# The end of a decoder step: the last down rows in smaller transfers, the last expert sums kept in PSUM, the output turned before it is normalised

## The reference

```python
h2 = rmsnorm(x, g_ffn) * (1 + sc2) + sh2
x = x + gt2 * moe(h2, w_router, b_router, w_gu, b_gu, w_d, b_d)   # 32 experts, 4 for each token
...
y_prompt = rmsnorm(xp, g_final)     # (1, 256, 1024)
y_sample = rmsnorm(xs, g_final)     # (8, 1, 1024)

def rmsnorm(x, g):
    y = x * lax.rsqrt(jnp.mean(x * x, axis=-1, keepdims=True) + RMS_EPS)
    return y * g
```

## Time and profile before

| | us |
|---|---|
| median of 3 runs | 1345.26 (1340.6 to 1347.05) |
| the profiled execution | 1347.29 |
| its span, first to last instruction | 1345.7 |
| PE busy | 1222.4 (91%) |
| DVE, ACT, POOL busy | 317.3, 175.4, 48.8 |
| moved by DMA | 500.51 MB, mean 372 GB/s |
| last weight transfer lands | 1304.48 |
| from there to the end of the span | 41.2 |

### The profile page before, as it was taken

The page is one execution under the profiler, slowest core; times in us unless marked ns, Lnnn a source line. Parts: engine busy times, 40 slices in busy tenths (PEclk is TensorE's granted clock), DMA queues, the critical chain, the costliest instruction groups (busy, mean ns, idle before and its releaser), DMA issues.

```text
span 1345.7 us, 15198 instructions
## 1 busy us (share of the span) xinstructions
PE 1222.4 (91%) x5950; PEld 608.0 (45%) x5950; DVE 317.3 (24%) x566; ACT 175.4 (13%) x341; POOL 48.8 (4%) x93
## 2 busy tenths in 40 slices
PE   5999998999999989899898989898998989898886
PEld 2788755688443433424242434334342424334234
DVE  2379855332112020111101110210111011102103
ACT  2132231100210100200010010001000100200002
POOL 0121231000000000000000000000000000000000
PEclk9899999999998999999999999998999999999988
DMA  9998999963699999999999999999999999999970
GB/s 353 328 349 302 376 314 364 395 261 138 250 422 414 373 417 409 418 406 420 407 413 414 419 415 418 418 415 420 380 421 415 392 415 420 417 416 419 403 296 34
DMA packets 105951, 500.51 MB, mean 372 GB/s; under 512 B 8514, under 2 KB 10672, under 8 KB 70161
## 3 DMA queue, kind: packets, MB, share of 16 engines
q1 hardware_dynamic: 99136, 478.37, 88.8%
q0 software_dynamic: 6496, 21.42, 4.6%
q10 hardware_dynamic: 272, 0.09, 0.0%
HBM read 496.48 MB, written 3.38 MB: 371 GB/s over the span
## 4 chain that ended last, share of the span: by engine, by line
PE 72%; DMA 23%; ACT 2%; DVE 1%; issue 1%; SPq 1%; DVEq 0%
PE ps L924 25%; DMA ring<-in_w_d 21%; PE ps L431 11%; PE ps L966 10%; PE ps L982 4%; PE ps L824 4%; PE ps L874 3%; PE ps L365 3%; PE ps L794 2%; PE ps L749 2%; DMA ring<-in_w_ada 2%; PE ps L396 1%; PE ps L605 1%; ACT oT L1265 1%; PE ps L890 1%
## 5 line engine op out<-in xcount | busy, mean ns | idle before, releaser
L924 PE MATMUL ps<-ring,zone 128*64 128x512 f32 x2032 | 443.0, 592 | 2.0 <-issue 2.0
L966 PE MATMUL ps<-ring,oT 128*64 128x512 f32 x1024 | 254.2, 654 | 73.5 <-DMA ring<-in_w_d 73.5
L924 PEld LDWEIGHTS ps<-ring,zone 128*64 128x64 f32 x2032 | 147.8, 137 | 289.2 <-issue 286.8
L966 PEld LDWEIGHTS ps<-ring,oT 128*64 128x64 f32 x1024 | 79.4, 150 | 247.4 <-issue 166.5
L1795 DVE TENSOR_SCALAR zone<-ps 128x1024 f32<-128x1024 f32 x16 | 19.6, 1225 | 631.3 <-PE ps L924 631.3
L431 PE MATMUL ps<-hT,ring 128*128 128x264 f32 x640 | 152.5, 397 | 2.1 <-DVE hT L1384 1.8
L431 PEld LDWEIGHTS ps<-hT,ring 128*128 128x128 f32 x640 | 123.1, 195 | 29.6 <-issue 6.6
L1260 ACT ACTIVATE attn<-zone 128x1024 f32<-128x1024 f32 x16 | 16.9, 1057 | 502.9 <-DVE zone L1795 502.8
L1812 DVE TENSOR_TENSOR zone<-zone,ps 128x264 f32<-128x264 f32 x64 | 27.5, 430 | 190.0 <-PE ps L982 190.0
L824 PE MATMUL ps<-zone,dec_scores 128*64 128x512 f32 x256 | 58.7, 599 | 0.0
L365 PE MATMUL ps<-ident,zone 128*128 128x128 f32 (+3 forms) x212 | 32.0, 277 | 15.9 <-DMA zone<-in_b_alpha 10.4
(11 more groups left out here) (340 smaller groups left out, 761.4 us busy)
## 6 DMA issues: line engine op xcount, KB each, us to landing
ring<-in_w_gu SPq DMA_DIRECT2D x127, 2048.0 KB, 17.6
ring<-in_w_d SPq DMA_DIRECT2D x64, 2048.0 KB, 15.6
ring<-in_w_ada SPq DMA_DIRECT2D x12, 2048.0 KB, 12.7
ring<-in_w_in SPq DMA_DIRECT2D x9, 2048.0 KB, 13.4
ring<-in_cache_k SPq DMA_DIRECT2D x32, 256.0 KB, 7.7
ring<-in_cache_k POOLq DMA_DIRECT2D x32, 256.0 KB, 6.7
ring<-in_cache_v SPq DMA_DIRECT2D x32, 256.0 KB, 10.5
ring<-in_cache_v POOLq DMA_DIRECT2D x32, 256.0 KB, 9.0
```

The costliest lines, as they stand in the source:

```text
L924: ins = pe.matmul(ps[64 * j:64 * j + CAP, c, :], xg[:, k, 2 * par + j, :], rows, start=False, stop=(k == KT - 1), skip_group_check=True)
L966: ins = pe.matmul(ps[64 * j:64 * j + CAP, 4 + c, :], hidT[:, k, j * CAP:(j + 1) * CAP], w[j][:, kk, c * 512:(c + 1) * 512], start=(k == 0) ...
```

## The change

The change rewrites all that follows the last quad, on four engines, in a function `finish` for each of PE, ACT and DVE, and `load_last` for SP.

- **Loads.** Of the last four `w_d` transfers, i = 0 and 1 stay. Instead of i = 2 and 3 (2 MB each), SP issues eight transfers of 512 KB, one for each of 4 row blocks and 2 experts, row block by row block, once both slots are free. PE waits for each row block alone (`late0` to `late2`, and `landed` for the last).
- **Sums in banks.** DVE adds `modT * acc` of the first seven quads to `xT` ahead of time, and clears banks 0 to 3 and 64 columns of bank 6. PE accumulates the last quad's sums in those banks: blocks m = 2b and 2b + 1 of the prompt in bank b (256 columns each), all sample columns in bank 6 (8 for each m). The products of par 0 and the samples' of par 0 come before `down(last, 1)`, those of par 1 behind it. DVE then does one operation for each m: `xT = ps * modT + xT`. `ye_tok[1]` is taken out in two halves, the first of them while PE computes the second.
- **g_final by rows.** PE spreads `g_final` over the partitions (`final_row`, two times four products of a broadcast column with the identity, bank 7), ACT copies it to `g_row`.
- **Output.** PE transposes `xT` (x2 unscaled) to token rows in banks 4, 5, 7, 0 (prompt) and 1, 2 (samples). ACT squares each bank with a sum along the row; DVE adds the two halves' sums, ACT takes the root (mean and epsilon within it), DVE the reciprocal, [128, 2] and [8, 1]. DVE then writes the output from the banks: bank times reciprocal of the token times `g_row`. SP stores in three transfers (256 tokens in two, then the samples), and the read of the number of rounds on DVE lies behind it.

The diff, without the removed lines that stand in the kernel above, and without the declarations of the new tiles (`g_row`, `squares_of`, `x2_ss`, `x2_inv`, `eps_col`, and `y_tok`, which lies over `hT`):

```diff
+        Y_BANKS = (4, 5, 7, 0, 1, 2)
...
-            def down(q, par, edge, cold):
+            def down(q, par, edge, cold, rnd=0):
 
                 n = q * 2 + par
                 if not cold:
                     pe.wait_ge(sig("ye_ready"), n)
                 for s in range(2):
                     pe.wait_ge(sig("read"), q * 10 + (5 + 2 * par + s))
-                    w = [expert_slot("dn", 2 * s + j, n, edge)[:, 0:4096].rearrange("p (k c) -> p k c", k=4)
-                         for j in range(2)]
+                    by_rows = edge and s == 1
+                    if by_rows:
+                        w = [ring[:, expert_load("dn", 2 * s + j, n, edge)[1], 0:4096]
+                             .rearrange("p (k c) -> p k c", k=4) for j in range(2)]
+                    else:
+                        w = [expert_slot("dn", 2 * s + j, n, edge)[:, 0:4096].rearrange("p (k c) -> p k c", k=4)
+                             for j in range(2)]
                     for kk in range(4):
                         k = 4 * s + kk
+                        if by_rows and kk < 3:
+                            pe.wait_ge(sig(f"late{kk}"), rnd * 32 + 32)
+                        elif by_rows:
+                            for j in range(2):
+                                expert_slot("dn", 2 * s + j, n, edge)
                         for c in range(2):
                             for j in range(2):
                                 ins = pe.matmul(ps[64 * j:64 * j + CAP, 4 + c, :], hidT[:, k, j * CAP:(j + 1) * CAP],
@@ -968,15 +980,76 @@
                                                 start=(k == 0), stop=(k == KT - 1), skip_group_check=True)
                                 if kk == 3 and c == 1:
                                     ins.then_inc(sig("slots_used"), 1)
-
-            def combine(q, last):
+                                elif by_rows and kk == 3:
+                                    ins.then_inc(sig("down_half"), 1)
+
+            def final_row(rnd, g):
+
+                if g == 1:
+                    pe.wait_ge(sig("g_taken"), rnd * 2 + 1)
+                for k in range(4):
+                    col = vecT[:, VEC_ROWS["g_final"][0] + 4 * g + k:VEC_ROWS["g_final"][0] + 4 * g + k + 1]
+                    ins = pe.matmul(ps[:, 7, k * P:(k + 1) * P], col.to_broadcast([P, P]), ident[:, :],
+                                    start=True, stop=True)
+                ins.then_inc(sig("g_filled"), 1)
+
+            def final_products(par, m):
+
+                return pe.matmul(ps[:, m // 2, (m % 2) * TP:(m % 2 + 1) * TP], ye_tok[par][:, m * P:(m + 1) * P],
+                                 putT[:, par, 0:TP], start=False, stop=(par == 1), skip_group_check=True)
+
+            def final_samples(par):
+
+                for m in range(KT):
+                    ins = pe.matmul(ps[:, 6, m * NS:(m + 1) * NS], ye_tok[par][:, m * P:(m + 1) * P],
+                                    putT[:, par, TP:T], start=False, stop=(par == 1), skip_group_check=True)
+                return ins
+
+            def final_turns(rnd, q):
+
+                for g in range(2):
+                    for t in range(2):
+                        for k in range(4):
+                            m = 4 * g + k
+                            if t == 0 and k % 2 == 0:
+                                pe.wait_ge(sig("added"), q * KT + (KT + m + 2))
+                            ins = transpose(ps[:, Y_BANKS[2 * g + t], k * P:(k + 1) * P],
+                                            xT[:, m, t * P:(t + 1) * P])
+                        ins.then_inc(sig("x2_turned"), 1)
+                pe.wait_ge(sig("x2_samples"), rnd + 1)
+                for g in range(2):
+                    for k in range(4):
+                        ins = transpose(ps[0:NS, Y_BANKS[4 + g], k * P:(k + 1) * P], xT[:, 4 * g + k, TP:T])
+                    ins.then_inc(sig("x2_turned"), 1)
+
+            def finish(rnd, q):
+
+                pe.wait_ge(sig("read"), q * 10 + 10)
+                final_row(rnd, 0)
+                pe.wait_ge(sig("sums_ready"), rnd + 1)
+                pe.wait_ge(sig("ye_ready"), q * 2 + 1)
+                for m in range(KT):
+                    final_products(0, m)
+                final_samples(0)
+                final_row(rnd, 1)
+                down(q, 1, True, False, rnd)
+                pe.wait_ge(sig("ye_half"), rnd + 1)
+                for m in range(KT):
+                    if m == 4:
+                        pe.wait_ge(sig("ye_ready"), q * 2 + 2)
+                    final_products(1, m).then_inc(sig("summed"), 1)
+                final_samples(1).then_inc(sig("samples_summed"), 1)
+                pe.wait_ge(sig("g_taken"), rnd * 2 + 2)
+                final_turns(rnd, q)
+
...
-                down(q + (QUADS - 1), 1, True, False)
-                combine(q + (QUADS - 1), True)
+                finish(rnd, q + (QUADS - 1))
...
+            def finish(rnd, q):
+
+                for g in range(2):
+                    act.wait_ge(sig("g_filled"), rnd * 2 + (g + 1))
+                    nc.scalar.activation(g_row[g], ps[:, 7, :], ACT.Copy).then_inc(sig("g_taken"), 1)
+                act.wait_ge(sig("sums_ready"), rnd + 1)
+                nc.scalar.activation(eps_root, eps_col, ACT.Sqrt)
+                act.wait_ge(sig("down_half"), rnd * 2 + 2)
+                nc.scalar.activation(ye_tok[1][:, 0:512], ps[:, 4, :], ACT.Copy).then_inc(sig("ye_half"), 1)
+                act.wait_ge(sig("slots_used"), down_done(q * 2 + 1, True))
+                nc.scalar.activation(ye_tok[1][:, 512:1024], ps[:, 5, :], ACT.Copy).then_inc(sig("ye_ready"), 1)
+                for n in range(6):
+                    rows = P if n < 4 else NS
+                    if n == 4:
+                        act.wait_ge(sig("x2_sums"), rnd * 2 + 1)
+                        nc.scalar.activation(x2_inv[:, 0:2], x2_inv[:, 0:2], ACT.Sqrt, bias=eps_col[:, 0:1],
+                                             scale=1.0 / D).then_inc(sig("x2_roots"), 1)
+                    act.wait_ge(sig("x2_turned"), rnd * 6 + (n + 1))
+                    nc.scalar.activation(squares_of[n], ps[0:rows, Y_BANKS[n], :], ACT.Square,
+                                         accum_out=x2_ss[0:rows, n:n + 1]).then_inc(sig("x2_sq"), 1)
+                act.wait_ge(sig("x2_sums"), rnd * 2 + 2)
+                nc.scalar.activation(x2_inv[0:NS, 2:3], x2_inv[0:NS, 2:3], ACT.Sqrt, bias=eps_col[0:NS, 0:1],
+                                     scale=1.0 / D).then_inc(sig("x2_roots"), 1)
+
...
-                add_quad(q + (QUADS - 1))
-                dve.wait_ge(sig("added"), q * KT + (QUADS * KT + KT))
+                finish(rnd, q + (QUADS - 1))
+
+            def finish(rnd, q):
+
+                for bank in range(4):
+                    ins = V.memset(ps[:, bank, :], 0.0)
+                V.memset(eps_col, EPS)
+                dve.wait_ge(sig("added"), q * KT + KT)
+                for m in range(KT):
+                    V.scalar_tensor_tensor(out=xT[:, m, 0:TP], in0=acc[:, m, 0:TP], scalar=modT[:, 40 + m, 0:1],
+                                           in1=xT[:, m, 0:TP], op0=ALU.mult, op1=ALU.add)
+                chain(V.tensor_tensor(acc[:, :, TP:T], acc[:, :, TP:T], modT[:, 40:40 + KT, 1:9], ALU.mult))
+                chain(V.tensor_tensor(xT[:, :, TP:T], xT[:, :, TP:T], acc[:, :, TP:T], ALU.add))
+                dve.wait_ge(sig("read"), q * 10 + 9)
+                V.memset(ps[:, 6, 0:KT * NS], 0.0).then_inc(sig("sums_ready"), 1)
+                for m in range(KT):
+                    if m % 2 == 0:
+                        dve.wait_ge(sig("summed"), q * KT + (KT + m + 2))
+                    V.scalar_tensor_tensor(out=xT[:, m, 0:TP], in0=ps[:, m // 2, (m % 2) * TP:(m % 2 + 1) * TP],
+                                           scalar=modT[:, 40 + m, 0:1], in1=xT[:, m, 0:TP], op0=ALU.mult,
+                                           op1=ALU.add).then_inc(sig("added"), 1)
+                dve.wait_ge(sig("samples_summed"), rnd + 1)
+                sums = ps[:, 6, 0:KT * NS].rearrange("p (k b) -> p k b", b=NS)
+                chain(V.tensor_tensor(qk_new, sums, modT[:, 40:40 + KT, 1:9], ALU.mult))
+                V.tensor_tensor(xT[:, :, TP:T], xT[:, :, TP:T], qk_new, ALU.add).then_inc(sig("x2_samples"), 1)
+
+                def inverse(rows, t0, n, first, number):
+                    dve.wait_ge(sig("x2_sq"), rnd * 6 + first + 2 * n)
+                    V.tensor_tensor(x2_inv[0:rows, t0:t0 + n], x2_ss[0:rows, first:first + n],
+                                    x2_ss[0:rows, first + n:first + 2 * n], ALU.add).then_inc(sig("x2_sums"), 1)
+                    dve.wait_ge(sig("x2_roots"), rnd * 2 + number)
+                    chain(V.reciprocal(x2_inv[0:rows, t0:t0 + n], x2_inv[0:rows, t0:t0 + n]))
+
+                def scaled(out, rows, t, n, g):
+                    V.scalar_tensor_tensor(out=out, in0=ps[0:rows, Y_BANKS[n], :], scalar=x2_inv[0:rows, t:t + 1],
```

(38 more changed lines are left out.)

65 lines of the change are left out of this document (21 added, 44 removed).

## The result

| | before | after |
|---|---|---|
| median (9 runs each) | 1345.4 (1340.6 to 1347.05) | **1333.38** (1331.8 to 1340.77) |
| the profiled execution, and its span | 1347.29, 1345.7 | 1335.32, 1333.7 |
| PE busy | 1222.4 | 1216.4 |

The ratio is 0.9932, 95% interval 0.9915 to 0.995: 0.7% faster. The forecast was 1333.9. The parts behind that agreement are less exact, and some of their errors cancel.

The account below looks back on a forecast made before the run. Weight stream and PE were nearly matched; the chain of waits behind the last quad decided. `down` ending at 1315.6 plus 18.65 gave 1334.3 against 1345.7, 11.4 less; off the median of 1345.26, 1333.9, range 1330 to 1340.

Parts of the forecast that it names:

- Hidden behind PE and buy nothing: Last `w_d` loads: row blocks land by 1304.5, or 1310.2 at the slow bound, before PE asks at 1313.9.
- rival 3: Last `w_d` loads: small transfers come one after the other, last landing at 1322.6, end 1342.8, no difference; chance 0.06.
- PE up to the end of `down`: PE from 1294.58: `final_row`, par 0 and sample products, then `down`; together 21.0 us, ending at 1315.6, 1.0 us later.
- no stop of more than a few tenths, clock 1.00 throughout: PE from 1294.6 on: busy without a gap to 1324.5 at full clock, instead of idling 3 us and running at half clock.
- Rival 1: Thin sample products lower PE's clock, slowing `down` or the transposes: one drop 1337 to 1337.5, both 1340.5; chance 0.12.
- E to the last prompt square: Behind `down`: par 1 and sample products, then transposes, fourth bank full after 8.85 us; ACT's last square adds 0.8.
- sum, root, reciprocal: Prompt output: DVE adds two sums (0.17), ACT root (0.21), DVE reciprocal (0.17), with three changes of engine: 0.75 us.
- four scalings: Prompt output: four DVE scalings of 512 columns out of PSUM, 0.74 each within bounds 0.69 and 0.95: 2.95 us.
- E to the end: From the end of `down` to the end of the span: 18.65 us, against 31.1 before.
- Transposes of x2: 32 passes: PE behind the last products: 32 passes at 0.1125 to 0.12 each, 3.6 us, and 0.2 for the drain.
- rival 2: Output: Square is not in the root's table set, so two more ACT loads of 1.28 us, 1336.4; chance 0.08.
- then the last stores, 3.0 as before: End of the span: the last stores take 3.0 us, unchanged from the kernel before.

Follow-up runs that it names:

- 3: The change with `combine` as before, all behind `down`, and sums kept in SBUF instead of banks: 1333.96, ratio 0.9918; second set 1330.59, ratio 0.9898.
- 7: The change without DVE's conditional block for further rounds (number of rounds still read): 1337.08, one execution.
- 2: The kernel before with only the loads by rows and their `late` waits: 1337.9, ratio 0.9966.
- 1, two-MB kernel: The change with the last `w_d` rows in 2 MB transfers and one wait: 1333.32, ratio 0.9923.
- 5: As 4, with the last six slots of `w_d` in 512 KB transfers, not the last two: 1327.19, ratio 0.9876.
- the change once more: The changed kernel unaltered, a second profile and set of times: 1334.21, ratio 0.9922.
- 6: The change with each set of thin sample products done three times, 48 thin passes instead of 16: 1350.15, one execution.
- SBUF kernel: The change with sums kept in SBUF instead of banks, run twice: 1333.96, ratio 0.9918, and 1330.59, ratio 0.9898.
- 4: As 3, with gate-matrix transposes and both `final_row` moved ahead of the last-but-one `down`: 1328.63, ratio 0.9888.
- 8: The kernel before, unaltered, a second profile: 1338.93, one execution.
- 9: The change, sums in banks kept, with gate transposes and `g_final` rows moved ahead of the last quad's first `down`: 1329.23, one execution.

## Why the prediction was right

Tails in one list (us): before 61.5, 59.6; loads by rows alone 55.3; change without sums in banks 45.8, 45.9; the change 51.2, 49.8, with 2 MB loads 51.2, without DVE's block 48.45. Read along it: removing stop and half clock is worth 6.2 or 4.3, by which profile of before is taken; the output part, the half-wise taking of `ye_tok[1]` and the rest another 9.5; the sums in banks give 2.3 of that back and the branch at the end of DVE 1.7 (3 and 7), and the last 1.4 of the profiled execution of after goes with its clock (1.7 up to the end of `down`). The 9.5 are a difference of two profiles (2 and the first of 3): 12.6 less behind `down` (31.1 and 18.45) and 3.2 more ahead of its end. Which part of the new output is worth how much of it was not run apart.

**Loads.** "Hidden behind PE and buy nothing": right, shown by 1. The rate of 410 GB/s, taken between 264 and 410, was right too (408 to 410), so rival 3 is out, here and with 24 such transfers in a row (5). The Trainium skill (DMA: Bandwidth & Descriptors, "Bandwidth") asks for transfers of 1 MiB or more for three quarters of the peak; the trace doesn't agree for transfers queued directly behind each other, where 512 KB kept the 408 to 410 GB/s of the 2 MB ones.

**PE up to the end of `down`.** Forecast 31.4 us behind the start of the tail. The kernel of 7 and the change once more have 31.6 (1318.64 - 1287.05 and 1314.62 - 1283.02), term by term within 0.3; the profiled execution of after has 33.3. The step "no stop of more than a few tenths, clock 1.00 throughout" failed there: `final_row(0)` and the products of par 0 cost 0.7 and 1.2 more, at a mean clock of 0.58 and 0.89. The clock fell at about 1293.5, before any thin sample product, behind the short pieces of PE between 1289.6 and 1292.95; with the same instructions it stayed at 1.00 in the change once more, whose windows of this stretch are:

```profile
1292.00:1294.00 2.00, 1.52 (x11) 1.07 (x11) 0.11 (x1) 1.00 (x3) 0.00 (x0) 1.00 1.05 418
1294.00:1296.00 2.00, 2.00 (x14) 1.82 (x13) 0.00 (x0) 0.60 (x1) 0.00 (x0) 1.00 1.03 408
```

It fell in the kernel after and in the two-MB kernel; it didn't in the change once more, in 6 and in 7, nor in the two SBUF profiles, which have the same instructions up to there. Why two of seven fell is open. Rival 1 named the wrong place. Its mechanism exists (6), but didn't show at 16 passes in any of the five profiles that have them.

**Behind `down`.** E is the end of `down`; all times from the chain above:

| term | forecast | after |
|---|---|---|
| E to the last prompt square | 9.65 | 8.30 |
| sum, root, reciprocal | 0.75 | 0.74 |
| four scalings | 2.95 | 2.73 |
| samples' sum, root, reciprocal | 0.8 | 0.60 |
| their two scalings | 1.5 | 1.39 |
| last stores | 3.0 | 4.14 |
| E to the end | 18.65 | 17.90 |

The first row holds the mis-sized term, "Transposes of x2: 32 passes". There are 16, done 1.8 us sooner; but PE then fills banks faster than ACT squares them, so ACT became the bound and 0.4 of it was lost again. The scalings came in their bounds (0.74 each), and overlap by a tenth. There is one table load of 1.28 us at 1302.57, under `down`, and none between squares and roots: rival 2 is out. The Trainium skill (ScalarE: Activation LUTs, "Table sets: the hidden batching unit") calls for batching by set; with Square and the root that had no price in any run here.

The last stores are the step that cost more, "then the last stores, 3.0 as before": 4.1, and 4.4 in the change once more. Not the stores are longer. The change put DVE's read of the number of rounds, and the branch on it, behind the output. The forecast took their 1.6 us off the path and gave them no price there; 7 shows that the branch now ends last, and gives 1.1 to 1.3 back.

**The sum.** 12.0 us between the medians against 11.4 forecast looks better than it is, and the closeness is in part luck: the tail of the profiled pair lost 10.3. `down` ended 1.9 later than forecast, most of it by the clock; 0.75 came back behind it; and the start of the tail, 1.7 us earlier, which was no part of the forecast, did the rest. Over the two profiles of each kernel the gain in the tail is 8.4 to 11.7. What holds is the mechanism: apart from the transposes, the clock and the end behind the last store, the terms of the new chain came within a few tenths of their prices.

## What to carry to other kernels

Cutting the last loads into pieces pays by what the compute engine waits for them, and by the clock that the wait may cost: it was worth 4 to 6 us alone, nothing once other work filled the wait, and some 2.5 us again when that work went elsewhere. Moving additions into PSUM accumulation isn't free when it splits one wide product into a wide and a thin one, since the thin one costs its weight load (a pass of 0.105 us for 8 columns against 0.22 for 256); here it lost 2.3 us. When a tail gets shorter, look at every engine's last instructions: a branch that nobody waited for was what the end waited for.

## What the runs showed of the hardware that was not expected

- **A clock that falls with PE busy.** 48 passes of 0.11 us each, back to back, and the clock was at about 0.5 for 3.5 us once and 6 us once (6), as it had been behind the 32 of the earlier trace rows. Stops of PE of 3.1 us brought it in some executions (4, 8) and not in others (the change once more, 9); one of 1.67 us (2) did not.
- **A taken branch costs 0.6 or 3 us on DVE.** From the branch over the block of further rounds to the next instruction: 2.8 to 3.2 us in the change, its repetition, the two-MB kernel, 6 and 9; about 0.6 in both runs of the SBUF kernel, in 4 and in 5. In each of the five long gaps the trace has one packet on an instruction queue, in none of the four short ones. For the kernel after, 1330.5 to 1333.4 (queue, kind: packets, MB, share):

```profile
q14 instruction: 1, 0.01, 1.0%
```

The Trainium skill (Runtime: NRT & Kernel Launch, "Instruction fetch mechanics") says that a taken branch to a page that isn't at hand waits for its fetch. The packets do not contradict it, but they show little: such a packet also comes within the 1.2 to 1.7 us behind each short gap, within the 2.8 us ahead of the branch in the kernel after, and near the end of the kernel of 7, which has no branch there. That the fetch is the cause, and why the target would be at hand in some kernels, is not shown.
- **Transposes in float32 are single instructions**, 0.117 us for 128 columns with the drain (24 in 2.82), 0.22 each at half clock (16 in 3.52).
